# Attention values turned around: two heads side by side in the columns of TensorE

## The chip, the core and the metric

One Trainium2 chip, one core of it. The core has a matrix engine (TensorE, PE in the rows), which multiplies a stationary operand of up to 128 x 128 that is loaded first (PEld) with a moving operand of up to 512 columns and writes to PSUM (8 banks of 512 float32 a partition); VectorE (DVE), ScalarE (ACT) and GpSimd (POOL), which work on SBUF and PSUM; and SyncE (SP), whose queue starts the DMAs. The engines run beside each other and wait for each other by semaphores. The metric is the device time of one execution in microseconds, the median of several runs.

## The reference

A decoder block over 1024 positions of width 1024, with a parallel mixer of two groups of 8 attention heads (head width 64):

```python
def dsa_attention(q, k, v, iq, ik, iw, k_top):      # 8 heads, sparse: top 256 keys of an indexer score
    ...
        logits = jnp.where(valid[:, None], logits, -jnp.inf)
        p = jax.nn.softmax(logits, axis=-1).astype(v.dtype)
        return jnp.einsum('bhqk,bqkhd->bqhd', p, v_sel)
def fox_attention(q, k, v, log_f):                  # 8 heads, causal, with a forgetting bias
    ...
        logits = jnp.where(causal[None, None], logits + bias, -jnp.inf)
        p = jax.nn.softmax(logits, axis=-1).astype(v.dtype)
        return jnp.einsum('bhqs,bshd->bqhd', p, v)
```

Around it stand the input projections (with rotary embedding), a root-mean-square norm of each group's output, the output projection, a SwiGLU network of width 2816, adaptive scales and shifts from `c @ ada_w`, and a last norm. All of it is float32.

## The kernel before

The kernel goes through stages: input projection with the indexer and the top-256 thresholds (to about 368 us in the profile), attention (368 to 650 us), output projection with the second norm (650 to 760 us), and the two halves of the feed-forward network, whose products are laid out by Strassen-like forms. This change touches attention and its two edges.

Attention runs 16 heads, first the 8 causal ones with forgetting (`hd` < `NH`), then the 8 sparse ones. A head has `TT` = 8 query tiles of 128 rows, so that a *unit* u = (head, t) covers queries of tile t and its t + 1 key tiles, and there are `UNITS` = 128 units. Each engine's program is written out by step s, in this order:

- PE, step s: `logits(s)` (lines 2207 to 2232: float32 rounded to one pass, two products, a high one of `KA` and a low one, `CK`/`CQ` with 68 rows for the causal heads, `KB` with 128 rows for the others), then the turns of the probabilities of unit s - 2 (`turn`, line 2207: 128 x 128 transposes by the identity into PSUM banks 4 and 5), then `values(s - 3)` (lines 2234 to 2245).
- `values(u)`: the turned probabilities `PT` are the stationary operand (128 keys x 128 queries), the values `Vn` of the head (64 columns) move. Both are full float32, and each of the t + 1 products shows as two weight loads and two matmuls in the trace. The output, 128 queries x 64, lands in bank 6 or 7.
- DVE, step s: `biased` (line 1701) adds the mask or bias and takes the row minimum, `lg_done`. Beside it DVE does, at fixed steps: `normalise(hd - 1)` at t = 3 (reciprocal of the sums, product from PSUM into `O`, lines 1717 to 1724), `query_lo(hd + 1)` at t = 5 (line 1652), one step of the adaptive modulation (`modulation`, line 1714) at t = 6, 7 for heads 4 and 5 and at t = 1, 2, 6, 7 for heads 6 to 11 and 13, squares in heads 12 and 15 and scaling in head 14.
- ACT, step s: copies of unit s - 2 from PSUM into `PT` (line 1153), then `expo(s)` (line 1158).
- POOL, head hd: `prepare(hd + 1)` (lines 850 to 864) rounds and splits the queries and keys `Qd`, `Kd` of the next head; it waits until the logits of head hd - 1 are done. In heads 12 to 14 it splits the rows of `w_out` (`split_out`).
- SP, iteration hd: `load_qk(hd + 2)` (four DMAs of 256 KB, line 606; `Qd` and `Kd` have two buffers each), then the `ada_w` rows of the modulation of head hd + 1 (512 KB each, line 659, each waiting until its buffer is free) and now and then a part of the values (`load_values`, line 597). The queue runs strictly in this order.

Semaphores that the steps below name: `pv_pe` counts finished value units, `tp_pe`/`tp_ev` turned groups written and copied, `k_lo`/`q_lo` finished splits of keys and queries, `md_done` steps of the modulation, `on_done` normalised outputs, `w_ready` split weights.

## Time and profile before

| | us |
|---|---|
| median of 3 runs | 1411.05 (1408.76 to 1412.88) |
| profiled execution, span of its instructions | 1410.2 |
| PE busy | 1348.2 (96%) |
| DVE busy | 1027.3 (73%) |
| POOL busy | 803.2 (57%) |
| ACT busy | 692.2 (49%) |

The spans of the profile are read from its page; the rows by stage come from the view of busy time by window, and the rows of single instructions from the view in order of time. Neighbouring instructions of one line are merged there into one row with their count, so the time from the start of one row to the start of the next, divided by the count, is the pace at which they are issued; the length of a matmul row includes the pipeline that drains behind it.

### The profile page before, as it was taken

The numbers are of one execution on the slowest core, as the hardware profiler recorded it, in microseconds if no ns is written. First come the engines' busy times: TensorE is split into PE (matmuls) and PEld (weight loads), VectorE is DVE, ScalarE is ACT, GpSimd is POOL, SyncE is SP. The second block draws the span as 40 slices with busy tenths as digits, with TensorE's granted clock in tenths as the row PEclk, the third lists the DMA queues.
The fourth block names the chain that finished last, engine by engine and source line by source line (L and its number), as shares of the span: only waits on it lengthen the run. The fifth ranks groups of instructions, "written<-read, shape, count | busy, mean of one in ns | idle before, by whom it ended". The sixth has DMA issues, their size and how long they took to land.

```text
span 1410.2 us, 20288 instructions
## 1 busy us (share of the span) xinstructions
PE 1348.2 (96%) x7043; PEld 1152.2 (82%) x7043; DVE 1027.3 (73%) x1599; ACT 692.2 (49%) x1372; POOL 803.2 (57%) x536
## 2 busy tenths in 40 slices
PE   1999999999999999999999899999999999999996
PEld 1988788888899999888888688888888888788885
DVE  4463779999685788996558777655566665579998
ACT  6523345563467667765335443444333333454545
POOL 0251312323336433580006798889998984798985
PEclk9999999999899999999999999999999999999998
DMA  9131222352333867432311233333223333998874
GB/s 384 43 97 60 90 68 75 105 167 91 115 81 103 261 196 208 123 117 90 120 46 45 60 112 113 112 112 112 97 98 112 113 108 132 369 381 293 279 240 161
DMA packets 126286, 200.59 MB, mean 142 GB/s; under 512 B 10637, under 2 KB 60997, under 8 KB 125162
## 3 DMA queue, kind: packets, MB, share of 16 engines
q1 hardware_dynamic: 126186, 199.30, 42.7%
q8 instruction: 57, 0.93, 0.3%
q14 instruction: 43, 0.35, 0.1%
HBM read 156.99 MB, written 42.27 MB: 141 GB/s over the span
## 4 chain that ended last, share of the span: by engine, by line
PE 82%; DVE 7%; issue 3%; DMA 2%; POOL 2%; ACT 2%; SPq 1%; ACTq 0%; DVEq 0%; POOLq 0%
PE PS L2047 21%; PE PS L2048 21%; PE PS L2049 21%; PE PS L2243 7%; PE PS L2207 4%; PE PS L2226 2%; DMA ada<-in_ada_w_dram 1%; PE PS L2228 1%; POOL WSf L937 1%; PE PS L2231 1%; DVE AS L1913 1%; DVE LP L1701 1%; POOL WS L949 1%; DVE junk L1731 1%; ACT F L1208 1%
## 5 line engine op out<-in xcount | busy, mean ns | idle before, releaser
L949 POOL TENSOR_TENSOR WS<-WSf,WS 128x512 fp32r<-128x512 f32 x109 | 161.6, 1490 | 9.1 <-ACT WS L1227 9.1
L1227 ACT CAST WS<-WSf 128x512 fp32r<-128x512 f32 x110 | 68.5, 623 | 196.2 <-POOL WSf L937 195.5
L937 POOL TENSOR_TENSOR WSf<-rawg 128x512 f32<-128x512 f32 x55 | 78.1, 1420 | 139.3 <-PE PS L2049 134.8
L2243 PE MATMUL PS<-Vn,PT 128*128 128x64 f32 x1152 | 144.2, 271 | 0.1
L2243 PEld LDWEIGHTS PS<-Vn,PT 128*128 128x128 f32 x1152 | 140.6, 194 | 0.9 <-ACT PT L1153 0.3
L2047 PE MATMUL PS<-yh,WS 128*128 128x512 f32 (+2 forms) x360 | 139.2, 387 | 1.5 <-DVE yl L1827 1.5
L2049 PE MATMUL PS<-yh,WS 128*128 128x512 f32 (+2 forms) x360 | 138.7, 385 | 0.0
L2048 PE MATMUL PS<-yl,WS 128*128 128x512 f32 (+2 forms) x360 | 138.7, 385 | 0.0
L2047 PE MATMUL PS<-BS,AS 128*128 128x512 f32 x308 | 120.4, 391 | 3.2 <-DVE BS L1918 2.1
L2049 PE MATMUL PS<-BS,AS 128*128 128x512 f32 x308 | 119.9, 389 | 0.0
L2048 PE MATMUL PS<-BS,AS 128*128 128x512 f32 x308 | 119.8, 389 | 0.0
L1158 ACT ACTIVATE LP<-LP,nmin 128x128 f32<-128x128 f32 (+7 forms) x128 | 99.7, 779 | 39.6 <-DVE nmin L1701 38.9
L1913 DVE TENSOR_TENSOR AS<-rawa,AS 128x512 fp32r<-128x512 f32 x77 | 102.2, 1345 | 23.1 <-ACT AS L1286 22.8
L2047 PE MATMUL PS<-XH,WS 128*128 128x512 f32 x264 | 103.6, 392 | 6.4 <-POOL WS L949 6.3
L1153 ACT COPY PT<-PS 128x512 f32<-128x512 f32 (+1 forms) x192 | 84.9, 476 | 44.3 <-PE PS L2207 43.2
L968 POOL TENSOR_TENSOR BS<-rawb,BS 128x512 fp32r<-128x512 f32 x57 | 89.5, 1575 | 28.0 <-ACT BS L1290 27.9
L1537 DVE TENSOR_SCALAR_CACHE_REDUCE marks_c<-sel,bis 128x640 f32<-128x640 f32 (+4 forms) x135 | 103.5, 819 | 0.6
L858 POOL CAST QT<-Qd 128x1024 fp32r<-128x1024 f32 x16 | 17.7, 1109 | 151.1 <-PE PS L2228 55.0
L2049 PE MATMUL PS<-XH,WS 128*128 128x512 f32 x264 | 103.5, 392 | 0.0
L2048 PE MATMUL PS<-XL,WS 128*128 128x512 f32 x264 | 103.3, 391 | 0.0
L961 POOL TENSOR_TENSOR rawb<-rawb 128x512 f32<-128x512 f32 x55 | 88.7, 1621 | 10.4 <-DMA rawb<-in_w_down_dram 10.2
L1082 ACT ACTIVATE PS<-sel,bis 128x896 f32<-128x896 f32 x64 | 67.6, 1056 | 50.0 <-DVE bis L1592 35.2
(321 smaller groups left out, 3732.0 us busy)
## 6 DMA issues: line engine op xcount, KB each, us to landing
rawb<-in_w_down_dram SPq DMA_DIRECT2D x132, 256.0 KB, 4.8
rawa<-gu_scratch SPq DMA_DIRECT2D x77, 256.0 KB, 4.7
gu_scratch<-GS SPq DMA_DIRECT2D x55, 256.0 KB, 4.7
raw<-in_w_in_dram SPq DMA_DIRECT2D x24, 512.0 KB, 3.9
rawg<-in_w_gate_dram SPq DMA_DIRECT2D x22, 512.0 KB, 4.3
rawu<-in_w_up_dram SPq DMA_DIRECT2D x22, 512.0 KB, 4.5
ada<-in_ada_w_dram SPq DMA_DIRECT2D x8, 1024.0 KB, 14.8
qk_scratch<-stage SPq DMA_DIRECT2D x32, 256.0 KB, 2.2
```

Of the source, the lines that this page charges most:

```text
L937: pool.tensor_tensor(WSf[m % N_SLOT][:], left(i, mat, a), left(i, mat, b), ALU.add if sign > 0 else ALU.subtract).then_inc(ws_sum, 1)
L949: pool.tensor_tensor(lo, WSf[m % N_SLOT][:] if b else left(i, mat, a), hi.bitcast(F32), ALU.subtract).then_inc(ws_ready, 1)
L961: pool.tensor_tensor(r[:, 0, :], r[:, 0, :], r[:, 1, :], ALU.add if RIGHT[DOWN[m // PAIRS]][2] > 0 else ALU.subtract).then_inc(gb_sum, 1)
L968: pool.tensor_tensor(b[:, 1, :], rawb[m % DOWN_RAW_B][:, 0, :], b[:, 0, :].bitcast(F32), ALU.subtract).then_inc(gb_lo, 1)
L1153: act.copy(PT[:, u % 2, b * BANK:b * BANK + w], src[:, 0:w]).then_inc(tp_ev, 1)
L1158: act.activation(LP[:, u % 3, 0:n], LP[:, u % 3, 0:n], ACT.Exp, bias=nmin[:, u:u + 1], scale=-1.0, accum_out=sums[:, u:u + 1]).then_inc(ex ...
L1537: did(dve.tensor_scalar(marks[0][:, n_tk % 2, 0:P * (t + 1)], view(t), limit, 0.0, op, ALU.add, accum_out=col(0, t)))
L1913: dve.tensor_tensor(AS[m % DOWN_SLOTS][:, 1, :], rawa[m % DOWN_RAW_A][:], AS[m % DOWN_SLOTS][:, 0, :].bitcast(F32), ALU.subtract).then_inc ...
L2047: pe.matmul(dst, left[0], right[0], start=first, stop=False)
L2048: pe.matmul(dst, left[0], right[1], start=False, stop=False)
L2049: return pe.matmul(dst, left[1], right[0], start=False, stop=last)
L2243: last = pe.matmul(PS[:, 6 + hd % 2, t * DH:(t + 1) * DH], PT[:, u % 2, j * P:(j + 1) * P], Vn[(hd // 4) % 2][:, j, cols], start=j == 0, s ...
```

## The change

The two factors of the value product change places, and two heads (a *pair*) are worked at once. `Vn` of the head, 128 keys x 64, is now stationary; the turned probabilities of **two** query tiles (256 columns, 128 at the diagonal) move. Head 2p writes partitions 0 to 63 of the output, head 2p + 1 partitions 64 to 127, so that each uses one half of the columns of the array. A pair has `PAIR_PRODUCTS` = 20 such steps, each for both heads. The output comes out transposed (head width x queries), is copied by ACT into `O` (`evac_output`), turned back by PE into the same bank (`turn_back`) and only then normalised by DVE, now by pair and half (`normalise(p, half)`).

The 20 products of a pair are laid in seven pieces (`VALUE_PARTS`) into steps 12, 14, 15, 17, 18, 22 and 23, counted from the start of the pair in which 16 steps are the pair's own units: 2, 1 and 3 products in tiles 4, 6 and 7 of the odd head, and 2, 3, 5 and 4 products in tiles 1, 2, 6 and 7 of the next even head. `PT` must hold far more probabilities (`pt_a`, `pt_b`), and to make room `Qd` and `Kd` lose their second buffers, `Vn` shrinks to one pair (rows of 512 bytes in its DMA, earlier 1 KB), the two `w_out` parts 3 and 2 are split after the last values instead of in head 14, and the modulation's fourth sum moves into `mod23`. `query_lo` moves from t = 5 to t = 4. Two turned outputs of the norm (`Y_EARLY`) go ahead of the last values. `load_qk(hd)` now waits for the split of head hd - 1 (`k_lo`, `q_lo` >= hd), earlier for that of head hd - 2.

```diff
-V_PARTS = 4
-V_HEADS = {5: 2, 9: 3}
-
-WO_HEAD = [12, 12, 13, 13, 13, 14, 14, 14]
+V_PARTS = 2
+PAIR = 2 * TT
+N_PAIR = NH
+N_GROUP = TT // 2
+PAIR_PRODUCTS = [(g, j) for g in range(N_GROUP) for j in range(2 * g + 2)]
+VALUE_PARTS = {(12, 2): 2, (14, 1): 1, (15, 2): 3, (17, 0): 2, (18, 0): 3, (22, 1): 5, (23, 2): 4}
+EVAC_AT = {PAIR * p + at: (p, half) for p in range(N_PAIR) for half, at in enumerate((17, 24))}
+BACK_AT = {PAIR * p + at: (p, half) for p in range(N_PAIR) for half, at in enumerate((20, 26))}
+NORM_AT = {PAIR * p + at: (p, half) for p in range(N_PAIR) for half, at in enumerate((23, 27))}
+LAST_STEP = PAIR * (N_PAIR - 1) + 28
+Y_EARLY = 2
...
+WO_ORDER = [0, 1, 4, 5, 6, 7, 3, 2]
+WO_HEAD = {0: 12, 1: 12, 4: 13, 5: 13, 6: 14, 7: 14}
...
+def value_plan():
+
+    plan, done = {}, 0
+    for (at, place), n in sorted(VALUE_PARTS.items()):
+        for p in range(N_PAIR):
+            plan[PAIR * p + at, place] = (p, PAIR_PRODUCTS[done:done + n])
+        done += n
...
-        PT = at(76, "PT", [P, 2, SEQ])
+        pt_a = [at(203, "PTa0", [P, 2 * P]), at(36, "PTa1", [P, 7 * P]), at(92, "PTa2", [P, 8 * P]), at(76, "PTa3", [P, 15 * P])]
+        pt_a_rest = {0: (1, at(39.5, "PTa0r", [P, P])), 2: (4, at(201.5, "PTa2r", [P, 3 * P]))}
+        pt_b = [at(196, "PTb0", [P, 11 * P]), at(148, "PTb1", [P, 15 * P])]
...
-        Qd = [at(172, "Qd0", [P, SEQ]), at(148, "Qd1", [P, SEQ])]
-        Kd = [at(176, "Kd0", [P, SEQ]), at(152, "Kd1", [P, SEQ])]
+        Qd = at(172, "Qd", [P, SEQ])
+        Kd = at(176, "Kd", [P, SEQ])
         turnF = [at(156, "turnF0", [P, SEQ]), at(160, "turnF1", [P, SEQ])]
         RX = [at(180, "RX0", [P, SEQ]), at(184, "RX1", [P, SEQ])]
         RT = [at(188, "RT0", [P, SEQ]), at(192, "RT1", [P, SEQ])]
-        Vn = [at(196, "Vn0", [P, TT, 4 * DH]), at(164, "Vn1", [P, TT, 4 * DH])]
+        Vn = [at(164, "Vn0", [P, TT, 2 * DH]), at(168, "Vn1", [P, TT, 2 * DH])]
+        wo_late = {3: at(120, "wolate3", [P, D]), 2: at(52, "wolate2", [P, D])}
...
+        def pt_write(hd, t, j0, j1):
+
+            home, first = pt_home(hd, t // 2, j0)
+            at0 = (j0 - first) * 2 * P + (1 - t % 2) * P
+            if j1 - j0 == 1:
+                return home[:, at0:at0 + P]
+            return home[:, at0:at0 + (2 * (j1 - j0) - 1) * P].rearrange("p (j c) -> p j c", c=P)[:, ::2, :]
...
+        def pt_read(hd, g, j):
+
+            home, first = pt_home(hd, g, j)
+            at0 = (j - first) * 2 * P
+            return home[:, at0:at0 + (2 * P if j <= 2 * g else P)]
...
+            def load_values(p):
+                cols = slice((p % 4) * 2 * DH, (p % 4 + 1) * 2 * DH)
+                if p >= 2:
+                    sp.wait_ge(pv_pe, N_GROUP * (p - 1))
+                for part in range(V_PARTS):
+                    tiles = slice(part * TT // V_PARTS, (part + 1) * TT // V_PARTS)
+                    src = v_dram[p // 4].rearrange("(t p) n -> p t n", p=P)[:, tiles, cols]
+                    sp.dma_start(Vn[p % 2][:, tiles, :], src).then_inc(qkv_in[p % 2], 16)
 
             def load_qk(hd):
...
-                if hd >= 2:
-                    sp.wait_ge(k_lo, hd - 1)
-                    sp.wait_ge(q_lo, hd - 1)
-                for i, dst in enumerate((Qd[b], Kd[b])):
+                if hd >= 1:
+                    sp.wait_ge(k_lo, hd)
+                    sp.wait_ge(q_lo, hd)
+                for i, dst in enumerate((Qd, Kd)):
...
+                if k in wo_late:
+                    sp.wait_ge(w_ready, N_PROJ + e - 1)
+                    sp.wait_ge(qk_pe, (2 * NH - 1) * TT)
+                    sp.dma_start(wo_late[k][:], w_out[k * P:(k + 1) * P, :]).then_inc(wo_in[e % 2], 16)
+                    return
...
                 load_qk(hd + 2)
-                if hd == 2:
-                    sp.wait_ge(md_ms, 3)
-                    for i, dst in enumerate((g1b[0:1, :], mod23[0:1, 0, :], mod23[0:1, 1, :], g2b[0:1, :])):
+                if hd % 2 and hd >= 3:
+                    load_values((hd + 1) // 2)
...
+                elif k == 7:
+                    pool.wait_ge(k_lo, 2 * NH)
+                    pool.wait_ge(q_lo, 2 * NH)
                 else:
-                    pool.wait_ge(k_lo, 9 + k)
-                    pool.wait_ge(q_lo, 9 + k)
-                split(N_PROJ + k, wo[k][:, 0, :], wo[k][:, 1, :], adar[:, k % 2, :]).then_inc(w_ready, 1)
+                    pool.wait_ge(pv_pe, N_PAIR * N_GROUP - (k == 3))
+                src = wo_late[k][:] if k in wo_late else adar[:, e % 2, :]
+                split(N_PROJ + e, wo[k][:, 0, :], wo[k][:, 1, :], src).then_inc(w_ready, 1)
...
-                    w = halves(P * (u % TT + 1))[b][1]
-                    if u >= 2 and b == 0:
-                        act.wait_ge(pv_pe, u - 1)
-                    act.copy(PT[:, u % 2, b * BANK:b * BANK + w], src[:, 0:w]).then_inc(tp_ev, 1)
+                    hd, t = divmod(u, TT)
+                    p, e = hd // 2, t // 2
+                    first, w = halves(P * (t + 1))[b]
+                    if hd % 2 == 0:
+                        held = N_GROUP * (p - 1) + e + 1
+                    else:
+                        held = N_GROUP * p + e - 1 if e >= 2 else N_GROUP * (p - 1) + e + 3
+                    if held > 0:
+                        act.wait_ge(pv_pe, held)
+                    j0, j1 = first // P, (first + w) // P
+                    if hd % 2 == 0 and t == 1:
+                        act.copy(pt_write(hd, t, 0, 1), src[:, 0:P])
+                        act.copy(pt_write(hd, t, 1, 2), src[:, P:2 * P]).then_inc(tp_ev, 1)
+                    elif j1 - j0 == 1:
+                        act.copy(pt_write(hd, t, j0, j1), src[:, 0:w]).then_inc(tp_ev, 1)
+                    else:
+                        act.copy(pt_write(hd, t, j0, j1), src[:, 0:w].rearrange("p (j c) -> p j c", c=P)).then_inc(tp_ev, 1)
+
+            def evac_output(p, half):
+                act.wait_ge(pv_pe, N_GROUP * p + 2 * half + 2)
+                act.copy(O[:, 4 * half:4 * half + 4, pair_cols(p)], PS[:, 6 + half, :].rearrange("p (t c) -> p t c", c=P)
+                         ).then_inc(ot_ok, 1)
...
+                if s in EVAC_AT:
+                    evac_output(*EVAC_AT[s])
+                if 2 <= s < UNITS + 2:
                     for b in range(len(halves(P * ((s - 2) % TT + 1)))):
                         evac_group(("T", s - 2, b))
+                if s == UNITS + 1:
+                    act.wait_ge(w_ready, N_PROJ + N_OUT - len(wo_late))
+                    for g in range(Y_EARLY):
+                        y_high(g)
...
-            def normalise(hd):
-                col = GW + hd * DH if hd < NH else (hd - NH) * DH
-                units = slice(hd * TT, (hd + 1) * TT)
-                dve.wait_ge(pv_pe, (hd + 1) * TT)
-                dve.reciprocal(rinv[:, units], sums[:, units]).then_inc(rv_ok, 1)
-                dve.wait_ge(rv_ok, hd + 1)
-                dve.tensor_tensor(O[:, :, col:col + DH], PS[:, 6 + hd % 2, :].rearrange("p (t d) -> p t d", t=TT),
-                                  rinv[:, units].unsqueeze(2).to_broadcast([P, TT, DH]), ALU.mult).then_inc(on_done, 1)
+            def normalise(p, half):
+                tiles = slice(4 * half, 4 * half + 4)
+                dve.wait_ge(back_pe, 2 * p + half + 1)
+                r, of = (v[:, PAIR * p:PAIR * (p + 1)].rearrange("p (a t) -> p a t", a=2)[:, :, tiles] for v in (rinv, sums))
+                dve.reciprocal(r, of).then_inc(rv_ok, 1)
+                dve.wait_ge(rv_ok, 2 * p + half + 1)
+                dve.tensor_tensor(O[:, tiles, pair_cols(p)].rearrange("p t (a d) -> p t a d", a=2),
+                                  PS[:, 6 + half, :].rearrange("p (t a d) -> p t a d", t=4, a=2),
+                                  r.rearrange("p a t -> p t a").unsqueeze(3).to_broadcast([P, 4, 2, DH]), ALU.mult
+                                  ).then_inc(on_done, 1)
...
-                if t == 3 and hd >= 1:
-                    normalise(hd - 1)
-                if t == 5 and hd + 1 < 2 * NH:
+                if t == 4 and hd + 1 < 2 * NH:
                     query_lo(hd + 1)
...
-            normalise(2 * NH - 1)
-            for g in range(KT // 2):
+            normalise(N_PAIR - 1, 0)
+            for g in range(Y_EARLY):
                 y_low(g)
-            dve.wait_ge(on_done, 2 * NH)
+            normalise(N_PAIR - 1, 1)
+            for g in range(Y_EARLY, KT // 2):
...
-            def values(u):
-                hd, t = divmod(u, TT)
-                pe.wait_ge(tp_ev, group_no[("T", u, len(halves(P * (t + 1))) - 1)] + 1)
-                if t == 0:
-                    pe.wait_ge(qkv_in[(hd // 4) % 2], 16 * V_PARTS * (hd // 8 + 1))
-                    if hd >= 2:
-                        pe.wait_ge(on_done, hd - 1)
-                cols = slice((hd % 4) * DH, (hd % 4 + 1) * DH)
-                for j in range(t + 1):
-                    last = pe.matmul(PS[:, 6 + hd % 2, t * DH:(t + 1) * DH], PT[:, u % 2, j * P:(j + 1) * P],
-                                     Vn[(hd // 4) % 2][:, j, cols], start=j == 0, stop=j == t)
-                last.then_inc(pv_pe, 1)
+            def turn_back(p, half):
+                pe.wait_ge(ot_ok, 2 * p + half + 1)
+                for i in range(4):
+                    last = pe.transpose(PS[:, 6 + half, i * P:(i + 1) * P], O[:, 4 * half + (i ^ 1), pair_cols(p)], ident[:])
+                last.then_inc(back_pe, 1)
+
+            def values(s, place):
+                p, products = value_at.get((s, place), (0, []))
+                for g, j in products:
+                    t = 2 * g + 1
+                    if j == 0:
+                        pe.wait_ge(tp_ev, group_no["T", PAIR * p + TT + t, len(halves(P * (t + 1))) - 1] + 1)
+                        if g == 0:
+                            pe.wait_ge(qkv_in[p % 2], 16 * V_PARTS * (p // 2 + 1))
+                        if p >= 1 and g % 2 == 0:
+                            pe.wait_ge(on_done, 2 * p - 1 + g // 2)
+                    n = 2 * P if j < t else P
+                    for a in range(2):
+                        rows = slice(a * DH, (a + 1) * DH)
+                        last = pe.matmul(PS[rows, 6 + g // 2, (g % 2) * 2 * P:(g % 2) * 2 * P + n], Vn[p % 2][:, j, rows],
+                                         pt_read(2 * p + a, g, j), start=j == 0, stop=j == t)
+                    if j == t:
+                        last.then_inc(pv_pe, 1)
...
-            for s in range(UNITS + 3):
-                hd, t = divmod(s, TT)
+            for s in range(LAST_STEP):
                 if s < UNITS:
                     logits(s)
+                values(s, 0)
                 if s in ANGLE_UNITS:
                     turn(("C", ANGLE_UNITS.index(s)))
                 if s in MOD_UNITS:
                     turn(("M", MOD_GROUP[MOD_UNITS.index(s)]))
-                if 2 <= s < UNITS + 2:
-                    for b in range(len(halves(P * ((s - 2) % TT + 1)))):
-                        turn(("T", s - 2, b))
-                if s >= 3:
-                    values(s - 3)
-
-
-            pe.wait_ge(tp_ev, len(plan))
+                n_turn = len(halves(P * ((s - 2) % TT + 1))) if 2 <= s < UNITS + 2 else 0
+                if n_turn:
+                    turn(("T", s - 2, 0))
+                values(s, 1)
+                if n_turn == 2:
+                    turn(("T", s - 2, 1))
+                if s == UNITS:
+                    for g in range(Y_EARLY):
+                        turn_y(g)
+                if s in BACK_AT:
+                    turn_back(*BACK_AT[s])
+                values(s, 2)
```

## Rows read from the trace of the kernel before

**Rows 1.** The page: span, busy time, and 40 equal slices of the span.

```profile
span 1410.2 us, 20288 instructions
PE 1348.2 (96%) x7043; PEld 1152.2 (82%) x7043; DVE 1027.3 (73%) x1599; ACT 692.2 (49%) x1372; POOL 803.2 (57%) x536
PE   1999999999999999999999899999999999999996
PEclk9999999999899999999999999999999999999998
```

**Rows 2.** Busy time by window: heads 0; 1; 2-5; 6-11; 9; 12; 13; 14; 15; end.

```profile
core 0: us, PE busy (x) PEld busy (x) DVE busy (x) ACT busy (x) POOL busy (x), PEclk, DMA share, GB/s
368.10:384.90 16.80, 15.50 (x79) 14.14 (x80) 7.30 (x18) 10.73 (x25) 9.04 (x9) 0.70 0.53 147
384.90:404.30 19.40, 18.46 (x147) 17.19 (x146) 14.85 (x24) 12.79 (x33) 9.32 (x9) 1.00 0.46 112
404.30:471.90 67.60, 67.36 (x545) 64.31 (x544) 44.49 (x85) 48.08 (x117) 37.95 (x23) 1.00 0.45 124
471.90:570.10 98.20, 98.20 (x794) 94.01 (x794) 84.49 (x139) 69.98 (x170) 33.08 (x20) 1.00 0.73 210
521.10:537.40 16.30, 16.30 (x134) 15.60 (x134) 13.83 (x24) 11.64 (x30) 5.33 (x4) 1.00 0.78 225
570.10:591.50 21.40, 20.66 (x153) 18.07 (x153) 21.30 (x35) 12.99 (x32) 15.16 (x8) 1.00 0.41 124
591.50:610.80 19.30, 18.97 (x156) 18.03 (x155) 16.52 (x27) 14.43 (x33) 8.98 (x5) 1.00 0.64 193
610.80:631.10 20.30, 19.75 (x146) 17.36 (x146) 20.20 (x28) 12.76 (x32) 19.70 (x11) 1.00 0.25 78
631.10:644.20 13.10, 13.10 (x105) 12.40 (x104) 9.96 (x34) 9.40 (x24) 0.00 (x0) 1.00 0.00 0
644.20:650.40 6.20, 6.20 (x59) 6.20 (x59) 0.45 (x2) 3.17 (x6) 0.00 (x0) 1.00 0.01 3
```

**Rows 3.** Order of time on PE at the last values: start, length, count.

```profile
647.26 3.46 PE L2243 MATMUL PS<-Vn,PT 128*128 128x64 f32 x30
650.55 1.04 PE L2294 MATMUL PS<-ident,O 128*128 128x128 f32 x8
```

**Rows 4.** Order of time on PE, a float32 product with 512 moving columns.

```profile
619.26 1.02 PE L2190 MATMUL PS<-g2b,ones 128*128 128x512 f32 x2
620.12 0.60 PE L2207 MATMUL PS<-ident,LP 128*128 128x128 f32 x4
620.56 0.22 PE L2243 MATMUL PS<-Vn,PT 128*128 128x64 f32 x1
```

**Rows 5.** Order of time on PE, four float32 products with one moving column.

```profile
596.95 1.00 PE L2193 MATMUL PS<-ones,mod 128*128 128x1 f32 x8
597.91 0.55 PE L2207 MATMUL PS<-ident,LP 128*128 128x128 f32 x3
```

**Rows 6.** Order of time on PE where 128 and 68 rows of the array alternate.

```profile
484.41 0.40 PE L2226 MATMUL PS<-KA,QT 128*128 128x512 f32 x1
484.64 0.40 PE L2228 MATMUL PS<-CK,CQ 68*128 68x512 f32 x1
484.88 0.82 PE L2207 MATMUL PS<-ident,LP 128*128 128x128 f32 x6
```

**Rows 7.** Order of time on DVE in head 9, units 1, 5 and on.

```profile
522.61 1.88 DVE L1714 SCALAR_TENSOR_TENSOR mod<-adax,cact,mod 128x1024 f32<-128x1024 f32 x1
...
531.02 1.22 DVE L1652 TENSOR_TENSOR QT<-Qd,QT 64x1024 fp32r<-64x1024 f32 x1
532.27 1.09 DVE L1701 CUSTOM_DVE_ANT_0 LP<-PS,sel 128x896 f32<-128x896 f32 x1
...
538.61 0.42 DVE L1701 CUSTOM_DVE_ANT_0 LP<-PS,sel 128x256 f32<-128x256 f32 x1 [0.88 <-PE PS L2231]
```

**Rows 8.** Order of time in SP's queue, the DMAs issued in head 9.

```profile
521.62 1.09 SPq L606 DMA_DIRECT2D Qd<-qk_scratch  x2
522.75 1.24 SPq L606 DMA_DIRECT2D Kd<-qk_scratch  x2
524.51 0.33 SPq L659 DMA_DIRECT2D adax<-in_ada_w_dram  x1
```

**Rows 9.** DMA issues in head 9: KB each, median us from issue to landing.

```profile
adax<-in_ada_w_dram SPq DMA_DIRECT2D x2, 512.0 KB, 6.5
Vn<-v_scratch SPq DMA_DIRECT2D x3, 256.0 KB, 6.5
```

**Rows 10.** Groups of ACT's instructions in head 9: count, busy us, mean ns.

```profile
L1153 ACT COPY PT<-PS 128x512 f32<-128x512 f32 x7 | 3.9, 578 | 0.9 <-PE PS L2207 0.8
```

More of the change, by code:

```diff
@@ L462, in build @@
         rv_ok = sem("rv_ok")
+        ot_ok = sem("ot_ok")
+        back_pe = sem("back_pe")
         on_done = sem("on_done")
@@ L645, in _ @@
                         load_piece(PIECES * (ch + 1) + t)
+                    if ch == 6 and t == 4:
+                        load_qk(1)
                 if ch == 4:
@@ L1164, in roots, with y_high @@
                                bias=epsc[:], scale=1.0 / GW).then_inc(yroot, 1)
-            for s in range(UNITS + 2):
+            def y_high(g):
+                k, half = Y_GROUPS[g]
+                cols = slice(half * BANK, (half + 1) * BANK)
+                act.wait_ge(yt_pe, g + 1)
+                act.activation(yh[:, k, cols], PS[:, y_bank(g), :], ACT.Identity, scale=gains[:, 1, k:k + 1]).then_inc(yt_hi, 1)
+            for s in range(LAST_STEP):
                 hd, t = divmod(s, TT)
@@ new lines, in turn_y @@
+            def turn_y(g):
+                k, half = Y_GROUPS[g]
+                pe.wait_ge(yn_ok, TT if k >= KT // 2 else TT + 4 * (half + 1))
+                if g < Y_EARLY:
+                    pe.wait_ge(lg_done, UNITS - 1)
+                elif g < Y_EARLY + 2:
+                    pe.wait_ge(tp_ev, len(plan))
+                elif g < Y_EARLY + 4:
+                    pe.wait_ge(on_done, 2 * N_PAIR)
+                else:
+                    pe.wait_ge(yt_lo, g - 3)
+                for i in range(4):
+                    last = pe.transpose(PS[:, y_bank(g), i * P:(i + 1) * P], O[:, 4 * half + i, k * P:(k + 1) * P], ident[:])
+                last.then_inc(yt_pe, 1)
@@ L2279, in _ @@
             dsa_rows, fox_rows = range(KT // 2), range(KT // 2, KT)
-            for g, (k, half) in enumerate(Y_GROUPS):
+            for g in range(Y_EARLY, 2 * KT):
                 if g == KT:
```

145 lines of the change are left out of this document (75 added, 70 removed).

## The prediction

> **What bounds the kernel now.** I read the page first. PE is busy in 96% of the span and in nearly every slice, at the full granted clock [rows 1], so a change has to take time from PE, in a stage in which no other engine stands close behind. Next, the busy time by window, cut at the heads (a head begins where DVE starts its first unit) [rows 2]. The reader should see three kinds of stretch. In heads 2 to 5 PE is busy 67.36 of 67.6 us and DVE only 44.49: PE alone is the bound. In heads 6 to 11 PE is busy all 98.2 us, but DVE is at 84.49, 14.1 a head of 16.4. In heads 12 and 14 DVE has 21.30 of 21.4 and 20.20 of 20.3: there DVE is the bound and PE may lose work for nothing. Last, the order of time on PE for the price of one product, and on DVE and SP for the timing of the q/k loads.
>
> **The value products on PE.** At the end, 30 value instructions go out in 650.55 - 647.26 = 3.29 us [rows 3], 0.11 us each, and a product has two, so 0.22. A pair of heads has 2 x 36 products: 15.8 us. With one moving column an instruction still takes (597.91 - 596.95) / 8 = 0.12 us [rows 5]: today the load of 128 stationary columns sets the pace and the 64 moving columns are almost free. The new form pays for moving columns. Two float32 instructions with 512 columns take 620.12 - 619.26 = 0.86 us [rows 4], so a product with 256 columns takes 0.43 and one with 128 takes 0.215. A pair has 16 of the first and 4 of the second for each head: 16 x 0.43 + 4 x 0.215 = 7.74 us per head. All now hangs on whether two heads in the two column halves stream together. The trace of before has no product that uses half the columns, so the bounds are 7.7 us (together) and 15.5 us (one after the other) per pair. I take together, because the two write separate partitions and hold separate weights, and keep the other end as a rival.
>
> Added around it, per pair: at each of the 7 pieces the second half starts one instruction later, 7 x 0.215 = 1.5 us. 14 changes between whole and half array: where 128 and 68 rows alternate, 512 columns follow each other in 0.23 us [rows 6], the same as their 0.215 of streaming but for 0.02, so a change may cost nothing; at most it drains a matmul, 0.22 us long [rows 4]. I take 0.08, 1.1 us. Eight turns back: 4 transposes take 620.56 - 620.12 = 0.44 us [rows 4], so 0.9 us. Sum 7.7 + 1.5 + 1.1 + 0.9 = 11.2 us against 15.8: PE gains 4.6 us a pair, 37 us in all. A pair of heads 6 to 11 goes from 32.7 to 28.1 us on PE, 14.05 a head, as much as DVE has. So at most half the nominal gain can show there, and after it DVE is next.
>
> The products are also uneven: 14 of 20 lie in the even head. With (32.7 - 15.8) / 2 = 8.45 us of other work, PE has 8.45 + 14 x 0.387 + 4 pieces x 0.37 + 0.44 = 15.8 us in an even head and 12.3 in an odd one.
>
> The Trainium skill (TensorEngine Tiling (Array Packing), Key Properties) says that changing the tiling mode drains TensorE. By the full drain above the 14 changes would cost 3.1 us a pair instead of 1.1, 16 us more of PE in all; rows 6 speak against it for row tiling, and no row here shows it for columns.
>
> **ACT, DVE, POOL.** ACT gains 16 copies of 512 columns, 0.58 us each [rows 10], one a head, beside 11.6 us of 16.3 in head 9 [rows 2]: hidden, in series only at the very end. The copies of probabilities write in strides, at the same size: nothing. DVE normalises the same elements in as many instructions: nothing. POOL has 5.3 us a head in head 9: the two late `w_out` splits fall after the last values, where PE has the output products of the other rows; hidden.
>
> **The q/k loads: the added wait.** `load_qk(hd + 2)` now waits for `query_lo(hd + 1)`, in tile 4 of head hd. Behind it in SP's queue stand the value loads (odd hd) and the modulation rows of the next head. The waiter is DVE in tile 1 of that head, and behind DVE everyone. In head 9 the first modulation row is issued 524.51 - 521.62 = 2.9 us after the first q/k load [rows 8] and lands 6.5 us later [rows 9]: 9.4 us. On the other side, `query_lo` ends at 532.2 and the modulation of the next head can start at 539.0, 6.8 us later [rows 7]; a unit earlier adds 1.0 and the idle time that goes takes 0.6: 7.2 us. DVE would wait 2.2 us. The queue will be emptier than today (nothing is issued from the head's end to tile 4), so I take 1.5 less: 0.7 us. For odd hd two value loads of 256 KB in 512-byte rows go ahead; no row has these; from their 0.43 us of issue each and about 1 us of transfer each I take 3 us. That wait falls in even heads, where DVE has 15.8 - 14.1 = 1.7 us to spare, so 1.3 shows. Three of each: 6 us, of which I count 5. Heads 0 to 5 have no such rows in tile 1: nothing.
>
> **The sum by stretch** [rows 2]. Heads 0 and 1 (36.2 us): head 0 has no values any more, then ACT with 10.7 us is next, 12.5; head 1 is held by DVE's 14.9, 16.0. Gain 7.7. Heads 2 to 5: two pairs x 4.6 = 9.2, less 1.2 for head 2, where DVE has 14.7: 8.0. Heads 6 to 11: three pairs of 15.8 + 14.1 = 89.7, a gain of 8.5, less 5 for the loads: 3.5. Heads 12 and 14: 0. Head 13, 19.3 with 16.5 of DVE: 17.5, gain 1.8. Head 15: 2.1 less on PE. The end loses: 14 products (12 x 0.43 + 2 x 0.215 = 5.6 us) with their edges of 0.8 stand where 3.3 us stood, and copy 0.6, turn back 0.4 and the rest of the way to DVE come before the outputs of bank 6 and 7 are free, less what the two early turns cover: 3.8 us later. Sum -7.7 - 8.0 - 3.5 - 1.8 - 2.1 + 3.8 = -19.3. The profiled span is 1410.2, so 1390.9; the median of the runs lies 0.85 above the span: **1392 us**. The later stages run on as they are, so the gain arrives at the end whole.
>
> **Rivals.**
> *The load loop binds (1403 us).* If the 9.4 us stand and the value loads cost 3, DVE waits 2.2 us in odd and 5.2 - 1.7 = 3.5 in even heads: 17 us in heads 6 to 11 instead of 5. For it: DMA is already at 0.78 in head 9 [rows 2]. Against: the queue has a pause before.
> *The halves go one after the other (1419 us, slower).* Then values cost 15.5 + 1.1 + 0.9 = 17.5 us a pair, 1.7 more than now. Heads 2 to 5 lose 3.4, heads 6 to 11 5.1, head 14 0.5, the end 8; heads 0, 1 and 13 still give 9.5 together: +7.5. It decides from the point at which a product of both heads takes over 0.75 us. Nothing in the trace excludes it; if loads show besides, up to 1440.
> *The loads show (1408 us).* A load of 128 columns alone takes 0.11 to 0.12 us [rows 5], of 64 half that; four per pair of products and none hidden: 20 x 0.22 = 4.5 us a pair, all that PE gained, and what is left is the shorter head 0. For it: today's values do pay for each load. Against: in rows 4 the 0.86 us are twice the columns' time, with both loads hidden. The Trainium skill (TensorE: Matmul & The Clock Gate, Part 3, The mechanism) says that a load overlaps a running matmul only where their row groups differ; here both heads use all rows, which gives this rival, and rows 4 disagree with the rule.
> *Better (1378 us).* No edge cost and no load wait: heads 6 to 11 at DVE's 84.5, 13.7 gained, heads 2 to 5 9.2, the end 1 lost: 33 us.
>
> **How the numbers follow.** Forecast, 1384 to 1400: 0.50. Better, 1374 to 1384: 0.10. Load loop, 1400 to 1408: 0.16. Loads show: 0.07. One after the other, 1414 to 1440: 0.17. 0.3%, or 4.2 us, is what a measurement here can tell from no change. Faster: 0.50 + 0.10 + 0.14 = 0.74. Same: 0.02 + 0.07 = 0.09. Slower: 0.17. The range of 1374 to 1424 holds all but the tails of the last and of the better case.
>
> **What would show it.** The value rows: starts of a pair of products 0.43 us apart say together, 0.86 one after the other. Heads 8 to 11 at 15 us alternate with 16; DVE in them waits for a DMA before the modulation row of tile 1, under 1 us in odd and about 3 in even heads. Head 0 near 12.5 us. Heads 12 and 14 unchanged. The end, from DVE's last unit to the first turned outputs of `O` in bank 6, some 4 us longer. I am wrong if PE is still busy in all of heads 2 to 5 with no shorter heads, or if DVE waits for DMAs beyond 2 us in every head.

## The result and the profile after

| | before | after | ratio (95% interval) |
|---|---|---|---|
| median, us (9 runs of each, side by side) | 1412.45 | 1406.18 | 0.994 (0.9921 to 0.996) |
| span of the profiled execution, us | 1410.2 | 1401.4 | |

Faster by 0.6%, about 8 us by the ratio; the forecast was 1392. The page of the kernel after, its first lines (those of before stand in [rows 1]):

```profile
span 1401.4 us, 19481 instructions
PE 1317.3 (94%) x6595; PEld 1073.5 (77%) x6595; DVE 1023.6 (73%) x1599; ACT 695.9 (50%) x1396; POOL 805.2 (57%) x536
```

PE has 30.9 us less to do, and the span is only 8.8 us shorter: the other 22.1 us became idle time of PE. Where it lies is read from the busy time by window, cut at the heads as in [rows 2]. The order is heads 0; 1; 2-5; 6-11; 12; 13; 14; 15; and from DVE's last unit to the first output product:

```profile
core 0: us, PE busy (x) PEld busy (x) DVE busy (x) ACT busy (x) POOL busy (x), PEclk, DMA share, GB/s
370.30:380.30 10.00, 7.79 (x45) 6.00 (x45) 7.30 (x18) 8.94 (x24) 8.04 (x6) 1.00 0.67 191
380.30:396.50 16.20, 13.38 (x96) 10.28 (x97) 11.23 (x23) 13.73 (x33) 5.35 (x4) 1.00 0.67 160
396.50:459.30 62.80, 58.55 (x431) 43.41 (x429) 50.38 (x85) 47.88 (x122) 44.03 (x24) 1.00 0.41 111
459.30:563.10 103.80, 94.25 (x640) 70.28 (x638) 85.81 (x140) 72.29 (x181) 31.06 (x20) 0.93 0.66 211
563.10:582.90 19.80, 18.95 (x131) 12.90 (x129) 18.74 (x37) 12.78 (x33) 15.25 (x9) 1.00 0.55 175
582.90:602.40 19.50, 16.32 (x120) 12.61 (x120) 16.10 (x26) 15.95 (x38) 12.91 (x7) 1.00 0.71 216
602.40:619.00 16.60, 15.14 (x104) 10.35 (x104) 16.12 (x29) 11.57 (x29) 12.03 (x7) 1.00 0.20 70
619.00:630.90 11.90, 11.27 (x81) 8.63 (x81) 9.92 (x33) 10.85 (x30) 0.00 (x0) 1.00 0.10 39
630.90:645.30 14.40, 13.45 (x119) 9.72 (x114) 5.46 (x14) 8.04 (x15) 6.75 (x4) 1.00 0.24 70
```

Against the spans of before, stretch by stretch, in us (forecast in brackets): heads 0 and 1 -10.0 (-7.7); 2 to 5 -4.8 (-8.0); **6 to 11 +5.6 (-3.5)**; 12 -1.6 (0); 13 +0.2 (-1.8); 14 -3.7 (0); 15 -1.2 (-2.1); end +3.3 (+3.8). The end of before is 644.15 to 655.24, where its first output product starts. The reader should see the row of heads 6 to 11: PE has 94.25 us of work in 103.80, where before it had 98.20 in 98.20, and the granted clock is 0.93 instead of 1.00. Attention begins 2.2 us later in this execution (in the nine profiles of the experiments it begins anywhere from 366.8 to 370.7 us), and what follows takes 1.2 us longer; I explain neither. Together: -8.8.

First the products. Order of time on PE in head 8: the last turns, a piece of four products (three with 256 moving columns, one with 128; each shows as two instructions a head) with its middle left out, and the first logits after it:

```profile
509.42 0.81 PE L2313 MATMUL PS<-ident,LP 128*128 128x128 f32 x6
510.16 0.43 PE L2359 MATMUL PS<-PTa,Vn 128*64 128x256 f32 x1
510.17 0.43 PE L2359 MATMUL PS<-PTb,Vn 128*64 128x256 f32 x1
510.43 0.38 PE L2359 MATMUL PS<-PTa,Vn 128*64 128x256 f32 x1
510.44 0.38 PE L2359 MATMUL PS<-PTb,Vn 128*64 128x256 f32 x1
510.64 0.38 PE L2359 MATMUL PS<-PTa,Vn 128*64 128x256 f32 x1
510.65 0.38 PE L2359 MATMUL PS<-PTb,Vn 128*64 128x256 f32 x1
...
511.62 0.27 PE L2359 MATMUL PS<-PTa,Vn 128*64 128x128 f32 x1
511.62 0.27 PE L2359 MATMUL PS<-PTb,Vn 128*64 128x128 f32 x1
511.83 0.33 PE L2332 MATMUL PS<-KA,QT 128*128 128x128 f32 x1
```

The two heads start 0.01 us apart and the next two instructions follow 0.21 us later: a product of both heads costs 0.43 us, as forecast for "together". From its first to its last start the piece loses nothing but the 0.05 us by which its second instruction is late (510.43 instead of 510.38).

Then the waits. What DVE waited for in heads 6 to 11, us in total, times, longest:

```profile
DVE LP L1798 <- PE PS L2337: 6.0, 11, 0.9
DVE mod L1813 <- DMA adax<-in_ada_w_dram: 4.5, 3, 2.4
DVE LP L1798 <- PE PS L2334: 4.2, 6, 1.1
DVE g1b L1813 <- DMA adax<-in_ada_w_dram: 2.7, 1, 2.7
```

The chain of waits in heads 7 and 8 (start, us, what) shows how the rows come late:

```profile
487.39 1.23 DVE QT L1749
...
488.69 0.45 SPq L663
...
491.11 0.58 SPq L654
...
492.28 6.62 DMA adax<-in_ada_w_dram
...
498.92 0.06 DVE mod L1813
```

`query_lo` (L1749) ends, SP issues the four q/k loads (L663), then the two value loads (L654), then the modulation row, and DVE starts on it 10.3 us after `query_lo` ended. That is the loop which the rival "the load loop binds" describes. In heads 6, 8, 9 and 10 DVE stands still for 2.7, 2.4, 1.1 and 1.1 us because of it. In heads 7 and 11 it waits for no DMA, and yet PE idles 2.0 and 2.3 us there. Head 11, on DVE and on POOL in order of time:

```profile
550.11 2.93 DVE L1813 SCALAR_TENSOR_TENSOR mod<-adax,cact,mod 128x1024 f32<-128x1024 f32 x1
```

```profile
548.71 3.24 POOL L926 TENSOR_TENSOR KB<-Kd,KA 128x1024 fp32r<-128x1024 f32 x1
```

DVE's instruction on a modulation row in tile 2 takes 2.93 us (2.86 in head 7) where the shortest take 1.28, beside a tensor-tensor instruction of POOL (L926), and PE waits for DVE behind it. So the late rows are not the only thing that holds heads 6 to 11.

### The profile page after: what moved, and what is told of

Same layout as the page of the kernel before. It is cut to its first block, busy times and chain, and to the rows that moved or that the text cites. A ratio compares the mean times of both kernels' runs of the same rounds, so it can differ in the third digit from the quotient of the medians.

```text
span 1401.4 us, 19481 instructions
## 1 busy us (share of the span) xinstructions
PE 1317.3 (94%) x6595; PEld 1073.5 (77%) x6595; DVE 1023.6 (73%) x1599; ACT 695.9 (50%) x1396; POOL 805.2 (57%) x536
## 3 DMA queue, kind: packets, MB, share of 16 engines
q1 hardware_dynamic: 130282, 199.30, 42.3%
## 4 chain that ended last, share of the span: by engine, by line
PE 76%; DVE 8%; issue 4%; DMA 4%; ACT 3%; POOL 2%; SPq 2%; DVEq 0%; ACTq 0%; POOLq 0%
PE PS L2153 21%; PE PS L2155 21%; PE PS L2154 21%; PE PS L2313 3%; PE PS L2359 3%; PE PS L2332 2%; DMA ada<-in_ada_w_dram 2%; DVE LP L1798 2%; DMA adax<-in_ada_w_dram 1%; DVE AS L2019 1%; POOL WSf L1006 1%; PE PS L2334 1%; DMA rawb<-in_w_down_dram 1%; PE PS L2337 1%; DVE mod L1813 1%
## 5 line engine op out<-in xcount | busy, mean ns | idle before, releaser
L2313 PE MATMUL PS<-ident,LP 128*128 128x128 f32 x576 | 92.9, 285 | 11.5 <-ACT PTa L1235 5.7
L2313 PEld LDWEIGHTS PS<-ident,LP 128*128 128x128 f32 x576 | 67.4, 144 | 37.4 <-ACT PTa L1235 13.3
L1030 POOL TENSOR_TENSOR rawb<-rawb 128x512 f32<-128x512 f32 x55 | 89.7, 1641 | 7.7 <-DMA rawb<-in_w_down_dram 7.7
L2332 PE MATMUL PS<-KA,QT 128*128 128x512 f32 (+1 forms) x192 | 78.8, 410 | 13.1 <-DVE nmin L1798 12.5
```

Of the source, the lines that this page charges most:

```text
L1030: pool.tensor_tensor(r[:, 0, :], r[:, 0, :], r[:, 1, :], ALU.add if RIGHT[DOWN[m // PAIRS]][2] > 0 else ALU.subtract).then_inc(gb_sum, 1)
L2313: last = pe.transpose(dst[:, i * P:(i + 1) * P], src, ident[:])
L2332: pe.matmul(dst, q, KA[i][:, b:b + w], start=True, stop=False)
```

## The experiments

My theory after the first look: the loop above takes the gain in heads 6 to 11; the products themselves do as forecast. The rivals: the value loads are the culprit (their place in the queue, or 512-byte rows); the halves of the array hinder each other; or DVE or ACT is the next bound and the loop costs nothing.

**Modulation rows first.** From head 5 on, the rows that the next head needs in its tiles 1 and 2 are issued ahead of the q/k loads; they need not wait for `query_lo`.

```diff
+                if hd >= 5:
+                    ahead = sum(h <= hd for h, _ in MOD_AT) + sum(h == hd + 1 and t < 4 for h, t in MOD_AT)
+                    while n_mod < ahead:
+                        load_mod(n_mod)
+                        n_mod += 1
                 load_qk(hd + 2)
```

> The changed kernel with one order altered in SP's queue: in heads 5 and on, the two modulation rows for tiles 1 and 2 of the next head are issued ahead of the q/k loads instead of behind them. If the load loop holds heads 6 to 11 (q/k load waits for query_lo, the rows stand behind it, DVE waits for the rows), these heads fall from 103.8 us to 94 to 97 us, no DVE wait on a modulation row is left, and the time against the kernel before goes from 0.994 to 0.987 to 0.990. If instead PE's uneven pieces and the sharing between DVE and POOL hold them, they stay at 102 to 104 us and the ratio at 0.994.

Measured: 1391.45 us (1388.32 to 1396.96), ratio 0.9855 (0.9823 to 0.9888); repeated with the later experiments 1391.40, ratio 0.9847 (0.982 to 0.9875). Heads 6 to 11:

```profile
457.60:549.40 91.80, 86.67 (x642) 64.69 (x641) 84.19 (x140) 70.26 (x181) 35.92 (x20) 1.00 0.75 224
```

103.8 us have become 91.8 (93.7 in the repetition), below the 94 to 97 expected; DVE waits for no DMA there, and the clock is whole again. So the order of SP's queue cost 10 to 12 us in this stage; without it the stage comes out 2.1 us (4.0) above the 89.7 that the prediction had for it without loads. Head 11 idles as before: its row beside POOL still takes 2.93 us, and PE idles 2.2 us there (2.1 in the repetition).

**Value loads last.** The same, and the value loads behind the modulation rows.

```diff
                 load_qk(hd + 2)
-                if hd % 2 and hd >= 3:
-                    load_values((hd + 1) // 2)
...
                     load_mod(n_mod)
                     n_mod += 1
+                if hd % 2 and hd >= 3:
+                    load_values((hd + 1) // 2)
```

> As e1_mods_first, and the two value loads of odd heads are issued after the modulation rows. If the value loads' 0.5 MB in 512-byte rows add to the wait, another 0 to 2 us go (ratio 0.986 to 0.989); if the rows of tiles 1 and 2 are already safe in e1, nothing changes.

Measured: 1391.97 us (1390.45 to 1399.43), ratio 0.9863 (0.983 to 0.9897), heads 6 to 11 in 91.9 us. Once the modulation rows are early, the place of the value loads is worth nothing.

**The wait alone, in the kernel before.** Nothing of the change but the stricter wait:

```diff
                 if hd >= 2:
-                    sp.wait_ge(k_lo, hd - 1)
-                    sp.wait_ge(q_lo, hd - 1)
+                    sp.wait_ge(k_lo, hd)
+                    sp.wait_ge(q_lo, hd)
```

> The kernel before, with only the wait of the change: load_qk(hd) waits for the splits of head hd - 1. Everything else, the two buffers too, is kept. Load loop: the modulation rows stand behind the wait here too, DVE waits 1 to 2 us for a row in each of heads 6 to 11, 98.2 us become 104 to 110, ratio 1.004 to 1.008. Rival (the wait is harmless, the rest of the change holds these heads): 98 us, ratio 1.000.

Measured: 1424.01 us (1418.69 to 1434.91), ratio 1.0093 (1.0058 to 1.0128). Heads 6 to 11 (busy time by window) and DVE's waits for DMAs there:

```profile
475.10:587.30 112.20, 104.68 (x784) 98.03 (x783) 88.81 (x140) 69.05 (x170) 32.51 (x19) 0.95 0.63 199
```

```profile
DVE mod L1714 <- DMA adax<-in_ada_w_dram: 6.3, 3, 3.0
DVE g2b L1714 <- DMA adax<-in_ada_w_dram: 2.3, 1, 2.3
DVE g1b L1714 <- DMA adax<-in_ada_w_dram: 2.2, 2, 1.4
```

The wait alone costs 14.0 us in six heads (98.2 to 112.2), more than I expected of it; the profiled execution was a long one (1430.69 us against the median of 1424.01), and by the ratio the whole kernel loses 13 us. DVE waits 10.8 us for rows, in all of the six heads but head 7. Not all of the 14.0 is waiting: DVE's busy time in the stage grows too, from 84.49 to 88.81 us, because modulation instructions that start later meet POOL's work (2.9 to 3.1 us in heads 6, 8, 9 and 11). The two parts add only roughly: 98.2 + 14.0 - 6.4 (the gain of the products as measured with the modulation rows first) = 105.8, measured 103.8. (With the forecast 8.5 in place of 6.4 the sum would come to 103.7; that is luck.) The loop is shown from both sides, by taking the rows out of it in the kernel after and by putting it into the kernel before.

**The late `w_out` splits alone, in the kernel before** (`WO_ORDER`, `WO_HEAD`, `wo_late` and what hangs on them).

```diff
-WO_HEAD = [12, 12, 13, 13, 13, 14, 14, 14]
+WO_ORDER = [0, 1, 4, 5, 6, 7, 3, 2]
+WO_HEAD = {0: 12, 1: 12, 4: 13, 5: 13, 6: 14, 7: 14}
```

> The kernel before, with only the order of the w_out splits of the change: parts 3 and 2 are split after the last values, six instead of eight in heads 12 to 14. If DVE in heads 12 to 14 was slowed by POOL's splits, heads 12 to 14 fall from 61.0 us by 4 to 5 us, with shorter square and scale instructions, and the ratio is 0.996 to 0.998. If head 14 got shorter because PE lost the values, it stays at 20.3 us here and the ratio at 1.000.

Measured: 1415.1 us (1406.87 to 1419.18), ratio 1.001 (0.9989 to 1.0031). DVE's scaling in head 14, before, in this experiment and after (count, busy us, mean ns):

```profile
L1742 DVE TENSOR_SCALAR O<-O,rstd 128x512 f32<-128x512 f32 x8 | 12.1, 1517 | 0.0
```

```profile
L1755 DVE TENSOR_SCALAR O<-O,rstd 128x512 f32<-128x512 f32 x8 | 8.2, 1031 | 0.0
```

```profile
L1843 DVE TENSOR_SCALAR O<-O,rstd 128x512 f32<-128x512 f32 x8 | 7.8, 973 | 0.0
```

With less of POOL beside it, DVE's scaling takes a third less, and head 14 falls from 20.3 to 17.2 us here and to 16.6 after. Heads 12 and 13 do not get shorter here (21.4 and 19.7 us), so the three together lose 2.7 us and not the 4 to 5 expected. In the kernel before, head 15 gives it back (13.1 to 15.7, PE busy throughout: its work had only been moved), net nothing. In the kernel after PE has less to catch up on, and head 14 keeps it: -3.7 us where I had forecast 0.

**The halves issued head by head.** In each piece all products of the even head first, then all of the odd one; everything else as after.

```diff
-                for g, j in products:
...
-                    for a in range(2):
-                        rows = slice(a * DH, (a + 1) * DH)
+                for a in range(2):
+                    rows = slice(a * DH, (a + 1) * DH)
+                    for g, j in products:
...
```

> The kernel after with one thing changed: in each of the seven pieces of a pair all products of the even head are issued first and then all of the odd head; the same instructions, another order. Theory: the two column halves stream side by side only because the two heads' instructions follow each other directly; issued head by head each product takes its own 0.43 us, so a pair pays 15.5 us instead of 7.7 for its values. That is 7.7 us more of PE a pair. Heads 2 to 5 have about 3 us of idle PE in them and get 12 to 15 us longer (62.8 to 75-78), heads 6 to 11 (103.8, of which PE is idle about 10) 14 to 20 longer, heads 12 to 15 5 to 10, the end 5 to 6: 1440 to 1455 us in all, and the starts of two successive instructions of one head 0.21 to 0.22 us apart with nothing of the other head between. Rival: the array's halves work through their own queues of instructions and run side by side whatever the order, at least across the boundary of the two heads in a piece; then the value rows of the second head start before the first head's have ended and the time stays within 10 us of the kernel after (1406).

Measured: 1415.89 us (1407.95 to 1421.13), ratio 1.0015 (0.9991 to 1.004): 0.75% slower than after by the two ratios, some 10.6 us (6 to 15 by their intervals), where strict order wanted 34 to 49. Order of time on PE in a piece of five products a head (two instructions each; ten of PTa and PTa2r are issued, then ten of PTb):

```profile
408.22 0.43 PE L2361 MATMUL PS<-PTa2r,Vn 128*64 128x128 f32 x2
408.49 1.24 PE L2361 MATMUL PS<-PTa,Vn 128*64 128x256 f32 x5
409.36 0.43 PE L2361 MATMUL PS<-PTb,Vn 128*64 128x128 f32 x2
409.57 0.38 PE L2361 MATMUL PS<-PTa,Vn 128*64 128x256 f32 x1
409.63 0.38 PE L2361 MATMUL PS<-PTb,Vn 128*64 128x256 f32 x1
409.79 0.38 PE L2361 MATMUL PS<-PTa,Vn 128*64 128x256 f32 x1
409.85 0.38 PE L2361 MATMUL PS<-PTb,Vn 128*64 128x256 f32 x1
410.00 0.38 PE L2361 MATMUL PS<-PTa,Vn 128*64 128x256 f32 x1
410.06 1.46 PE L2361 MATMUL PS<-PTb,Vn 128*64 128x256 f32 x6
```

The odd head's first product starts at 409.36, when the even head still has three instructions to start (409.57, 409.79, 410.00) and one that has just begun: the other half starts ahead of three instructions that stand before it in the program. Between its first and last start this piece takes 2.92 us, against 1.79 in the kernel after; a piece of two products takes 0.6 in both. Neither side of my expectation holds as written. In this piece and in those of three products (first instruction of the odd head at 395.55 and 401.06, again ahead of three) the halves are independent, but not over more than that, so here a pair of heads had to be interleaved, or laid in pieces of two products (four instructions), to stream together. One after the other throughout would have cost this piece twice the after value, 3.6 us. What sets the reach of three I did not find out.

**Two reasons for heads 2 to 5.** There PE's busy time fell by 67.36 - 58.55 = 8.8 us, what the prediction wanted (9.2), but the spans fell by 4.8. In the odd heads 3 and 5 PE is busy 12.8 of 14.0 and 12.4 of 14.8 us. In head 5 of the kernel after, on DVE and on POOL in order of time:

```profile
450.17 3.51 DVE L1749 TENSOR_TENSOR QT<-Qd,QT 64x1024 fp32r<-64x1024 f32 x1
```

```profile
447.85 2.38 POOL L926 TENSOR_TENSOR CK<-Kd,KA 64x1024 fp32r<-64x1024 f32 x1
450.19 2.39 POOL L941 TENSOR_TENSOR RX<-RX,RT 128x1024 f32<-128x1024 f32 x1
452.55 3.36 POOL L942 TENSOR_TENSOR RX<-RX,RT 128x1024 f32<-128x1024 f32 x1
```

`query_lo` takes 3.51 us where it takes 1.22 in the kernel before [rows 7]; it ends at 453.68, 1.1 us after POOL's L941 has ended (452.58), and POOL's L942 then takes 3.36 instead of 2.38. From 450.19 to 455.91 the three instructions take 5.7 us; alone they take 2.38 + 1.22 + 2.38 = 6.0, so one of the two engines works while the other waits. The Trainium skill (SBUF — State Buffer, Who interferes with whom) says that a DVE instruction with two inputs in SBUF contends with a GpSimd instruction that reads SBUF, over a shared pair of ports that is locked exclusively; these rows agree. In heads 2 to 5 `query_lo` loses 8.1 us in this way. In the kernel before it met POOL in none of them: POOL's preparation began 2.0 to 3.2 us before the start of heads 3 to 5 (419.56, 435.97, 452.37); now it waits for the single buffer of `Kd` and begins 0 to 1.9 us behind it (413.39, 429.29, 444.88), and `query_lo` has moved towards it. First experiment, on top of "modulation rows first" (`q_lo` of this head awaited before the rotary embedding of heads 3 to 5):

```diff
                     if hd + 1 in ROPE_HEADS:
+                        pool.wait_ge(q_lo, hd + 2)
                         rotate(ROPE_HEADS.index(hd + 1))
```

> The base plus one wait on POOL: in heads 3, 4 and 5 the rotary embedding's two tensor-tensor instructions start only when query_lo of that head is done. In the base query_lo takes 4.46, 3.00 and 3.73 us in these three heads instead of 1.22, and each time it ends about 1.2 us after a tensor-tensor instruction of POOL has ended, as if the one had to wait for the other to finish. Theory: that is the missing gain of heads 2 to 5; query_lo moved a unit earlier and POOL's work moved later with the single buffer of Kd, so that they meet. Then query_lo takes 1.2 to 2.2 us in these heads, and heads 3 to 5 (46.9 us in the base) get 2 to 4 us shorter, unless the modulation rows of heads 4 and 5 now wait for POOL instead. Rival: what holds these heads is the way from PE over DVE and ACT back to PE with the few value products of an odd head, and query_lo only fills idle time; then heads 3 to 5 stay within 0.7 us.

Second, ACT's copy of the turned outputs behind that step's copies of probabilities:

```diff
-                if s in EVAC_AT:
+                if s in EVAC_AT and s % PAIR == 1:
                     evac_output(*EVAC_AT[s])
...
+                if s in EVAC_AT and s % PAIR == TT:
+                    evac_output(*EVAC_AT[s])
```

> The base with one reordering on ACT: at the start of an odd head the copy of the pair's second half of outputs (0.56 us) is issued after the copies of that step's turned probabilities, not before. Theory: this copy is not hidden, as the prediction had it: PE waits 1.08 us at the start of head 5 (and 1.1 in head 3) for the copies behind it, and each odd head gets 0.5 us shorter where PE is next to be the bound, heads 3, 5 and 7 above all; 1 to 2.5 us in all. Rival: DVE's chain sets these heads, the wait on PE is idle time that costs nothing, and the time stays within 0.7 us.

Third, both together.

> Both edits of the last two on the base. If both theories hold, the gains add: 3 to 6 us less than the base, about 1387 us. If neither, the same as the base.

Measured, in one sequence on one chip with the base at 1391.40 (1389.47 to 1393.09):

| | median, us | runs from to | ratio to before |
|---|---|---|---|
| rope waits | 1385.95 | 1380.27 to 1388.29 | 0.9803 (0.9772 to 0.9833) |
| copy after | 1393.47 | 1391.04 to 1395.88 | 0.9862 (0.9835 to 0.9888) |
| both | 1390.89 | 1386.53 to 1391.07 | 0.9834 (0.9805 to 0.9863) |

Heads 3 to 5, first of the base, then with the rope's wait:

```profile
408.90:455.60 46.70, 41.70 (x301) 30.71 (x300) 36.02 (x61) 34.48 (x87) 35.65 (x20) 1.00 0.52 146
```

```profile
415.70:457.50 41.80, 41.58 (x311) 31.59 (x310) 30.65 (x62) 36.19 (x90) 33.89 (x20) 1.00 0.61 170
```

These heads are 4.9 us shorter, `query_lo` takes 1.22, 1.22 and 1.44 us in them, DVE has 5.4 us less, and PE is busy all but 0.2 us: the first theory holds for these heads, by more than the 2 to 4 us expected. With both edits they are as short (42.3 us). (Heads 1 and 2, ahead of the edit, were 4.8 us longer in that profile than in the base's, which shows how much single heads vary from execution to execution; the ranges of the medians' runs do not touch.) The copy's place brings nothing: heads 3 and 5 are 13.9 and 14.8 us instead of 15.0 and 15.0, and the whole is not faster. PE's wait of 1.1 us for ACT at the start of an odd head is one that costs nothing, or it is given back; with both edits 4.9 us of the rope's 5.4 are lost again. Heads 6 to 11 show where (88.4 us with the rope's wait alone, 92.3 with both): it is head 11, 13.5 against 16.6 us, and head 9, 14.3 against 15.4. In both heads the modulation row of tile 2 takes 2.93 us with both edits and 1.5 to 1.6 with the rope's wait alone. In head 11 that long row stands in each of the five other profiles with the modulation rows first, and behind it the granted clock falls in four of them, not in the fifth. So the rope's wait is shown to free heads 3 to 5, but that all of its 5.4 us come from there is not shown; why the row in head 11 misses POOL in one execution stays open.

The kernel with the modulation rows first and the rope's wait beats both kernels: 2.0% below before, 1.4% below after.

## Why the prediction was right and wrong

**Values on PE: right, a little too dear.** "Together" holds (0.43 us a product of both heads). Over all pieces the values take 68.3 us, 8.5 a pair, where 7.7 of streaming and 1.5 for edges were put. There is no such edge: the prediction took the second half to start one instruction late, 0.215 us, and it starts 0.01 late. The mode changes cost about 0.1 us on each side (last turn to first value 0.20 instead of 0.11; last value to logits 0.21 instead of 0.11), near the 0.08 that I took. (8.5 is worked out from the starts of the 640 value instructions: from the first to the last of each piece, and 0.215 for the last.) So PE does what its sum said: -8.8 us of busy time in heads 2 to 5.

**The rule on loads.** At 0.21 us an instruction of 256 columns, the rows above leave no room for a load: loads of a half array are hidden under products that use the same rows. The Trainium skill (TensorE: Matmul & The Clock Gate, Part 3, The mechanism), by which a load overlaps a running matmul only where their row groups differ, does not describe this kernel; the rival that rested on it, 1408 us, came near the measured time for another reason.

**The load wait: the failed step.** I had the mechanism and its place, and the waits of DVE were shorter than I took them: 0.7 us in an odd and 3 in an even head were forecast (for the even one its own working, 2.2 - 1.5 + 3, gives 3.7), 11 in all, and 0 to 1.1 and 1.1 to 2.7 were measured, 7.2 in all. Yet 9.1 of the 10.5 us by which the profiled span missed the sum are this stage's. What failed is the term of the sum, "6 us, of which I count 5" (for which 5 and not 6 the prediction has no reason). Measured against the stage with the modulation rows first it is 12 us (103.8 - 91.8; 10 against the repetition). The two rows of the stage say what it consists of. PE idles 9.55 us instead of 5.13, which is 4.4 more and near my 5. And PE is busy 94.25 us instead of 86.67 with the same work, which is 7.6 more: this part I had put at nothing, because I took PE's time for a given work as fixed. It is not: the clock falls four times in heads 6 to 11, and four times 1.7 us are 6.8 of the 7.6 (last section). Without the loads the stage is also 2.1 us above the 89.7 of the sum; PE still idles 1.1 to 2.3 us in the odd heads, where a modulation row of tile 2 takes 1.8 to 2.9 us instead of 1.28 beside POOL. How many of the four falls are the loads' own is not shown: two are in heads 7 and 11, where DVE waited for no DMA. The rival "the load loop binds" had the size of the stage nearer, 17 us instead of 5 (so 1404 and not the 1403 it gives), but from waits of 2.2 and 5.2 us that did not occur.

**The moved `query_lo`: costed at nothing, and not nothing.** The prediction moved it a unit earlier and counted only the gain of 1.0 us of lead. It did not ask what POOL does at that time once its input comes later. It cost about half the gain of heads 2 to 5: 4.0 us of the busy time that PE lost there did not show in the spans, and 4.9 came back in heads 3 to 5 with the rope's wait.

**Heads 0 and 1**: 2.3 us more gain than forecast, and up to half of the 10.0 is the clock's. The row of head 0 before [rows 2] has a granted clock of 0.70: it stands at its lower level from 371 to 381 us, after PE had idled 1.4 us, so (1 - 0.70) x 16.8 = 5.0 us of PE's work are lost there. After, PE idles 1.5 us from 370 to 373 and the clock stays at 1.00. The prediction says "at the full granted clock" and has no term for this; why it falls in the one and not in the other is open. ACT, which the prediction took as head 0's next bound with 10.73 us, has only 8.94 after. Neither point was tried in an experiment. **Heads 12 and 14**: 0 was wrong. "DVE is the bound" was right, but DVE's own instructions got shorter: in head 14 when POOL's work left; in head 12 the squares took 1285 ns instead of 1791 on average, which the late splits alone did not give (1790), so that the 1.6 us there stay unexplained. **Head 13**: 1.8 less was forecast, and it takes 0.2 more. PE has 2.65 us less to do there but idles 3.2 us, of which 2.9 waiting for ACT's copies of probabilities; ACT, which the prediction put at nothing here, has 15.95 us in the head instead of 14.43. No experiment was made on it. **Head 15 and the end**: the sum of both was forecast at +1.7, measured +2.1. **Later stages**: as they were, within 1.2 us.

**Luck.** Heads 0, 1, 12 and 14 together gave 7.6 us more than forecast, for reasons that the prediction does not have. Without them the profiled span would be only 1.2 us shorter than before, and the change would show as no change.

## What to carry to other kernels

An engine's row that is "not the bottleneck" still sets when the next load may be issued. Where a buffer is given up, follow the queue of the issuing engine past the new wait to every transfer behind it, and put what can go early in front of the wait: that one reordering was worth more than the whole change (12 to 13 us by the ratios, against 8). And when an instruction is moved in time, look at what DVE and POOL would then do at once: here DVE's instructions with two inputs in SBUF and POOL's took about the sum of their times (5.7 us for 2.38, 1.22 and 2.38), not the longer one. Last, count more than the wait: here 4.4 us of added idle time came together with 7.6 us of slower work on PE.
